# Query and key projections of the first block computed with dims on partitions, and their rotary turn made there

## The reference, cut to what matters

```python
proj = jnp.einsum('bsd,de->bse', xn, w_in)
q_a, k_a, v_a, q_r, k_r, v_r, g_r, gate_logits = jnp.split(proj, IN_SPLIT_POINTS, axis=-1)
def apply_rotary(t, cos, sin):
    t1, t2 = jnp.split(t.astype(jnp.float32), 2, axis=-1)
    c = cos[None, :, None, :]
    s = sin[None, :, None, :]
    return jnp.concatenate([t1 * c - t2 * s, t1 * s + t2 * c], axis=-1)
...
for g, (window, dilation) in enumerate(ATTN_PAIRS):
    o, l = dilated_window_attention(q_a[:, :, g], k_a[:, :, g], v_a[:, :, g], dilation, window // (2 * dilation))
...
mix_w = jax.nn.softmax(jnp.stack(lses, axis=0), axis=0)
y_att = jnp.einsum('gbsh,gbshd->bshd', mix_w, jnp.stack(outs, axis=0)).reshape(B, S, ATTN_OUT_W)
```

## Time and profile before

| | |
|---|---|
| median of 3 runs | 2767.23 us (2767.2 to 2769.93) |
| profiled execution | 2768.16 us, its span 2766.3 us |
| TensorE busy | 2609.0 us, 94% |
| VectorE, ScalarE, GpSimd busy | 1219.6, 880.6, 852.4 us |
| the four mixers end at | about 382 us of the span |

### The profile page before, as it was taken

The page is one execution under the profiler, slowest core; times in us unless marked ns, Lnnn a source line. Parts: engine busy times, 40 slices in busy tenths (PEclk is TensorE's granted clock), DMA queues, the critical chain, the costliest instruction groups (busy, mean ns, idle before and its releaser), DMA issues.

```text
span 2766.3 us, 36753 instructions
## 1 busy us (share of the span) xinstructions
PE 2609.0 (94%) x14332; PEld 1850.0 (67%) x14332; DVE 1219.6 (44%) x2420; ACT 880.6 (32%) x1671; POOL 852.4 (31%) x1166
## 2 busy tenths in 40 slices
PE   9999999999988888888888899999999999999999
PEld 7888777888533333334333367788888887888887
DVE  6433745225633333333333357553441565644422
ACT  4433335322211111111111144553332446433332
POOL 5343434552000000000000043345555435345554
PEclk9999999999999999999999999999999999999999
DMA  4223222336999999999999951122332221123322
GB/s 159 79 100 105 72 76 77 104 122 257 414 427 427 428 429 428 429 429 429 428 428 428 426 178 66 50 92 92 94 115 95 90 100 61 62 91 106 108 92 76
DMA packets 128151, 571.99 MB, mean 207 GB/s; under 512 B 11152, under 2 KB 58640, under 8 KB 102928
## 3 DMA queue, kind: packets, MB, share of 16 engines
q1 hardware_dynamic: 122768, 560.82, 51.0%
q10 hardware_dynamic: 5248, 9.32, 1.1%
HBM read 565.86 MB, written 4.26 MB: 206 GB/s over the span
## 4 chain that ended last, share of the span: by engine, by line
PE 68%; DMA 23%; DVE 5%; ACT 2%; issue 1%; POOL 0%; SPq 0%; ACTq 0%; DVEq 0%
PE ps L392 43%; DMA wide<-in_moe_w 16%; PE ps L1577 8%; DMA arena<-in_moe_w 7%; PE ps L2105 3%; PE ps L2084 2%; PE ps L2074 1%; PE ps L2125 1%; PE ps L673 1%; PE ps L708 1%; PE ps L689 1%; PE ps L2091 1%; PE ps L1353 1%; PE ps L937 0%; POOL ring_r L349 0%
## 5 line engine op out<-in xcount | busy, mean ns | idle before, releaser
L349 POOL TENSOR_TENSOR ring_r<-ring,ring_r 128x256 fp32r<-128x256 f32 (+2 forms) x1136 | 833.7, 773 | 1818.3 <-ACT ring_r L332 1818.3
L392 PE MATMUL ps<-xnT_r,ring_r 128*128 128x512 f32 (+1 forms) x1664 | 483.9, 374 | 0.0
L392 PE MATMUL ps<-ring_r,xnT_r 128*128 128x512 f32 (+1 forms) x1296 | 412.7, 389 | 3.0 <-DVE xn_r L3171 2.5
L392 PEld LDWEIGHTS ps<-xnT_r,ring_r 128*128 128x128 f32 x1664 | 304.4, 188 | 56.6 <-issue 1.3
L392 PE MATMUL ps<-ring_r,arena_r 128*128 128x512 f32 x1392 | 323.9, 391 | 0.0
L392 PE MATMUL ps<-xn_r,ring_r 128*128 128x512 f32 (+1 forms) x832 | 310.2, 373 | 0.0
L332 ACT ACTIVATE ring_r<-ring 128x1024 fp32r<-128x1024 f32 (+2 forms) x284 | 272.4, 1025 | 88.7 <-DMA ring<-in_w_down 67.4
L392 PEld LDWEIGHTS ps<-ring_r,arena_r 128*128 128x128 f32 x1392 | 259.9, 188 | 56.4 <-issue 2.2
L392 PEld LDWEIGHTS ps<-ring_r,xnT_r 128*128 128x128 f32 x1296 | 251.0, 200 | 49.9 <-issue 5.7
L2105 PE MATMUL ps<-wide,arena 128*32 128x512 f32 x752 | 192.0, 657 | 90.5 <-DMA wide<-in_moe_w 90.5
L2105 PEld LDWEIGHTS ps<-wide,arena 128*32 128x32 f32 x752 | 51.8, 118 | 229.5 <-issue 210.8
(11 more groups left out here) (407 smaller groups left out, 3491.2 us busy)
## 6 DMA issues: line engine op xcount, KB each, us to landing
wide<-in_moe_w SPq DMA_DIRECT2D x143, 2048.0 KB, 32.9
arena<-in_moe_w SPq DMA_DIRECT2D x46, 2048.0 KB, 32.9
ring<-in_w_in SPq DMA_DIRECT2D x22, 2048.0 KB, 8.3
ring<-in_w_up SPq DMA_DIRECT2D x20, 2048.0 KB, 8.6
ring<-in_w_down SPq DMA_DIRECT2D x10, 2048.0 KB, 7.8
ring<-in_w_in SPq DMA_DIRECT2D x16, 512.0 KB, 4.9
ring<-in_w_out SPq DMA_DIRECT2D x4, 2048.0 KB, 8.5
ring<-in_w_ret_branch SPq DMA_DIRECT2D x2, 2048.0 KB, 9.0
```

The source lines that it names most:

```text
L349: ins = nc.gpsimd.tensor_tensor(ring_r[:, q % 2, piece], ring[:, q % 2, piece], ring_r[:, 2 + q % 2, piece].bitcast(F32), ALU.subtract)
L392: ins = nc.tensor.matmul(bank, left, right, start=(start and k == 0), stop=(stop and k == 2))
```

## The change

Six projections, all query and key ones but the first mixer's query and the last mixer's key, become "crossed" jobs: the weights are the stationary operand and all 512 tokens the moving one, so that job b gives dims 128b to 128b+127 of all tokens, already turned. Their rots go. ScalarE first copies the four groups of 32 partitions, halves of a head swapped, into `X.swapped` (`swap_crossed_act`); then VectorE multiplies them by a sine table, multiplies the bank by the cosine table, and adds both into `qT` or `kT` (`rotate_crossed_dve`). The two tables of 512 columns, 512 KB together, are loaded into `rows[:, 3]` ahead of unit 1. The turn back of a tile stands six chunks after the values (before: directly behind them). From unit 1 on, high copies stand at chunk 5 of the second job and chunks 1, 3 and 5 of the third.

```diff
+        BACK = 6
...
-                            if 2 <= p <= pairs and tile_of_pair(self.attention, p - 2) is not None:
-                                yield "back", tile_of_pair(self.attention, p - 2)
...
-                        if pairs and off == 2 and p == pairs + 1:
-                            yield "back", NT - 1
+                        if pairs and off == BACK and 2 <= p <= pairs + 1 and tile_of_pair(self.attention, p - 2) is not None:
+                            yield "back", tile_of_pair(self.attention, p - 2)
...
+                    if toks == CROSSED:
+                        ins = products(ps[:, dense_bank(e), :], [xnT_high[:, c, :], h_low[:, c, :]], [w[:, c, i * P:(i + 1) * P] for w in chunks_of_unit(u)],
+                                       weights_left=True, **flags)
...
+        def rotate_crossed_dve(v, M, e, n):
...
+            v.wait_ge(Z.turned, M.rots0 + sum(r < n for r in M.roped) - (x == 0))
+            v.wait_ge(halves_swapped, y + 1)
+            nc.vector.tensor_tensor(swapped, swapped, X.sin_T, ALU.mult)
+            nc.vector.scalar_tensor_tensor(out=rot, in0=ps[:, dense_bank(e), :], scalar=M.scales[way], in1=X.cos_T, op0=ALU.mult,
+                                           op1=ALU.mult).then_inc(Z.taken_dve, 1)
...
+            nc.vector.tensor_tensor(dst, rot, swapped, ALU.add).then_inc(rotated, 1)
...
+        def swap_crossed_act(a, M, e, n):
...
+            a.wait_ge(Z.proj_ready, M.jobs0 + n + 1)
+            if y >= 2:
+                a.wait_ge(rotated, y - 1)
...
+            half = DH // 2
+            for at in range(0, P, half):
+                other = at ^ half
+                ins = nc.scalar.activation(X.swapped[y % 2][at:at + half], ps[other:other + half, dense_bank(e), :], ACT.Copy, scale=scale)
+            ins.then_inc(halves_swapped, 1)
+
+        HIGH_AT = ((1, 5), (2, 1), (2, 3), (2, 5))
...
-                    if i == 2 and c % 2:
+                    if u == 0 and i == 2 and c % 2:
                         high_act(a, u + 1, (c // 2,))
+                    elif u and (i, c) in HIGH_AT:
+                        high_act(a, u + 1, (HIGH_AT.index((i, c)),))
...
+            at, n = TABLES["rope_t"]
+            sp.dma_start(rows[:, 3], const[:, at:at + n]).then_inc(rope_loaded, 16)
```

More of the change, by code:

```diff
@@ L107, in tables @@
     parts["rel"] = np.concatenate([rel, from_middle * np.ones((P, 1))], 1)
+    turns = (np.arange(S, dtype=np.float32)[None] * np.tile(inv, P // inv.size)[:, None]).astype(np.float32)
+    signs = np.where(p % DH < DH // 2, -1.0, 1.0)
+    parts["rope_t"] = np.concatenate([np.cos(turns), signs * np.sin(turns)], 1)
     at = 0
@@ L592, in build @@
             assert lay.at == ARENA
+            cos_T, sin_T = rows[:, 3, 0:S], rows[:, 3, S:]
             merged_top = small[:, 32:64].rearrange("p (i h) -> p i h", i=NT)
@@ L612, in build @@
         FIRST_HALF, SECOND_HALF, WHOLE = slice(0, HALF), slice(HALF, P), slice(0, P)
-        ENDS = "ends"
+        ENDS, CROSSED = "ends", "crossed"
         end_tokens = extra_r[:, 0:2 * KC * P].rearrange("p (x c t) -> p x c t", x=2, c=KC)
@@ L818, in __init__ @@
                 self.attention, self.first, self.apart, self.leaves, self.merges = attention, first, apart, leaves, merges
-                self.roped = [n for n, (kind, _, _, _) in enumerate(jobs) if kind != "v"]
+                self.crossed = [n for n, job in enumerate(jobs) if job[3] == CROSSED]
+                self.roped = [n for n, job in enumerate(jobs) if job[0] != "v" and n not in self.crossed]
+                self.by_dve = sorted(self.roped + self.crossed)
                 self.entries = []
@@ L864, in steps @@
                         yield "merge", k - 3
-                assert not pairs or self.first + self.apart * (pairs + 1) + 2 < at
+                assert not pairs or self.first + self.apart * (pairs + 1) + BACK < at
             def job(self, e):
@@ L892, in mixer_of @@
             values = [ENDS] + [SHIFTED[i] for i in range(1, NT)] if g == 0 else [tokens(i, True) for i in range(NT)]
-            jobs = [(kind, base + j, i, tokens(i, False)) for j, kind in enumerate("qk") for i in range(NT)]
+            jobs = [(kind, base + j, i, tokens(i, False) if base + j == 0 else CROSSED) for j, kind in enumerate("qk") for i in range(NT)]
             jobs += [("v", base + 2, i, toks) for i, toks in enumerate(values)]
@@ L902, in mixer_ret @@
         def mixer_ret():
-            jobs = [(kind, U_REST + j, i, tokens(i, False)) for j, kind in enumerate("qvkv") for i in range(NT)]
+            jobs = [(kind, U_REST + j, i, CROSSED if kind == "q" else tokens(i, False)) for j, kind in enumerate("qvkv") for i in range(NT)]
             dsts = [X.vr_low[:, i, :] for i in range(NT)] + X.vr_high
@@ L948, in mixer_pe @@
                         pe.wait_ge(Z.turned_kept, M.rots0)
+                        pe.wait_ge(rotated, M.crossed0)
                         pe.wait_ge(Z.taken_act, M.acts0)
@@ L1008, in mixer_dve @@
                         last_merge_dve(v, link, k)
+        def rotate_crossed_dve(v, M, e, n):
+            x = M.crossed.index(n)
+            y = M.crossed0 + x
+            kind, _, b, _ = M.jobs[n]
+            way = "qk".index(kind)
+            rot, swapped = X.rot[:, x % 2, :], X.swapped[y % 2]
+            v.wait_ge(Z.proj_ready, M.jobs0 + n + 1)
+            if y == 0:
+                v.wait_ge(rope_loaded, 16)
+            v.wait_ge(Z.turned, M.rots0 + sum(r < n for r in M.roped) - (x == 0))
[3 more added lines that the diff above has]
+                                           op1=ALU.mult).then_inc(Z.taken_dve, 1)
+            v.wait_ge(Z.taken_dve, M.dves0 + M.by_dve.index(n) + 1)
+            dst = M.heads[way][:, b, :]
+            if M.permuted:
+                rot, swapped = (z.rearrange("p (k r) -> p r k", r=STRIDE) for z in (rot, swapped))
+                dst = dst.rearrange("p (r k) -> p r k", r=STRIDE)
+            nc.vector.tensor_tensor(dst, rot, swapped, ALU.add).then_inc(rotated, 1)
+            v.wait_ge(rotated, y + 1)
+        def swap_crossed_act(a, M, e, n):
+            y = M.crossed0 + M.crossed.index(n)
+            scale = M.scales["qk".index(M.jobs[n][0])]
+            a.wait_ge(Z.proj_ready, M.jobs0 + n + 1)
+            if y >= 2:
+                a.wait_ge(rotated, y - 1)
+            elif y == 0:
+                a.wait_ge(Z.roped, M.rots0 + len(M.roped))
+            half = DH // 2
[4 more added lines that the diff above has]
+        HIGH_AT = ((1, 5), (2, 1), (2, 3), (2, 5))
         def mixer_act(a, M):
@@ L1030, in mixer_act @@
                             a.wait_ge(Z.probs_turned, sum(len(chunks_of(g)) for g in ORDER))
+                            a.wait_ge(rotated, M.crossed0 + len(M.crossed))
                             at, n_rel = TABLES["rel"]
@@ L1035, in mixer_act @@
                         nc.scalar.activation(dst, ps[:, dense_bank(e), :], ACT.Copy).then_inc(Z.taken_act, 1)
+                    elif c == KC - 1 and M.entries[e][1] in M.crossed:
+                        swap_crossed_act(a, M, e, M.entries[e][1])
+                        if M.before is None and M.entries[e][1] == 2 * NT - 1:
+                            decays_act(a, 1)
                 elif what == "rot":
                     m = M.entries[k][1]
+                    way = "qk".index(M.jobs[M.roped[m]][0])
                     a.wait_ge(Z.turned, M.rots0 + m + 1)
-                    dst, src = M.heads[m // NT], ps[:, dense_bank(k), :]
+                    dst, src = M.heads[way], ps[:, dense_bank(k), :]
                     if M.permuted:
@@ L1318, in rest_pe @@
                         pe.wait_ge(Z.turned_kept, last.rots0 + len(last.roped))
-                        pe.wait_ge(Z.taken_act, last.acts0 + len(last.jobs) - len(last.roped))
+                        pe.wait_ge(rotated, last.crossed0 + len(last.crossed))
+                        pe.wait_ge(Z.taken_act, last.acts0 + len(last.jobs) - len(last.by_dve))
                     if s_ >= 2:
```

60 lines of the change are left out of this document (32 added, 28 removed).

## The result

The changed kernel takes 2784.81 us (median of 4 runs, 2784.12 to 2792.2), the kernel before 2767.22 beside it: the ratio is 1.0067, 95% interval 1.0055 to 1.008. It is 17.6 us slower; the forecast was 2770 in a range that ended at 2779.

A forecast was written before the change was run, and what follows sets the result against it. TensorE was taken as the only engine on the chain. Rots removed, waits in the second, third and last mixer: -10.6 + 1.9 + 1.9 + 9.6 = +2.8 us, arriving whole, so 2770 us, range 2762 to 2779.

The forecast's parts named there:

- What is removed: TensorE's chain in the mixers: 24 of 32 rots go at 0.44 us each, 10.6 us saved.
- 96 x 0.272: TensorE, the removed transposes: if each gave back its whole duration, 26.1 us would go and the sum end at 2754.
- The four copies: ScalarE, each crossed job: four copies of 32x512 take about 2.07 us, upper bound 2.34, lower 0.6.
- If the copies step by 0.6 or more: ScalarE's groups of 32x512: a sign that the forecast is wrong; it expected steps of 0.5 us.
- The rotation: VectorE, each crossed job: two multiplications and an addition take 2.2 us, bounded by 2.1 and 2.6.
- The waits of the middle mixers: Second and third mixer, values of pairs 1 and 2: TensorE waits 0.3 and 1.5 us, 1.9 us per mixer.
- The prediction's own walk: Queues walked through the second mixer: 1.9 us of waits; with copies of 2.34 and rotation of 2.6 it ends at +10.
- rival 2: Second and third mixer: ScalarE and VectorE in lockstep become the bound from copies of about 2.25 us, 2773 to 2781, chance 0.33.
- The last mixer: Values wait for the late merge: 3.7 us for tile 0, 3.1 tile 1, 2.7 tile 2, 0.1 last tile; sum 9.6.
- The clock is no part of the answer: TensorE in the stretches that the change touches: the granted clock is 1.00, so it gets no term.
- The banks, the table, the rest: Second mixer's start waits 0.7 us, the 0.61 behind the last goes, these cancel; 1.3 us of table load is hidden.
- The high copies: From unit 1 on: left in place they would cost some 2 us; the new, earlier place costs nothing.

The follow-up runs named there:

- e3: The changed kernel with one ScalarE copy of 128x512 for the four, halves not swapped (result not the reference's): 2769.53 us, 1.0003.
- e10: The changed kernel with the last mixer as before and the halves swapped on VectorE straight from the bank, without ScalarE: 2767.35 us, 0.9992.
- e12: The changed kernel with the last addition in natural token order, so tokens are wrongly ordered in the first two mixers: 2787.70 us, 1.0057.
- e4: The changed kernel with 20 short products that nothing reads ahead of each of the last mixer's three waits: 2785.00 us, 1.0056.
- e5: The changed kernel with 9 short products that nothing reads ahead of the waits at the values, middle mixers included: 2781.97 us, 1.0051.
- e13: e10 with the dense banks going on in turn from one mixer to the next: 2764.81 us, 0.9989.
- e11: The changed kernel with the high copies back in the third job's odd chunks: 2798.80 us, 1.0099.
- e1: The changed kernel with the turns of the last mixer alone back at their old chunks: 2775.89 us, 1.0026.
- e6: The changed kernel with the last mixer as before, its query uncrossed and its turns at the old place: 2778.05 us, 1.0038.
- e8: The changed kernel with a tile's merge issued at its turn back instead of at the end of the job: 2780.70 us, 1.0043.
- e2: The kernel before with only the turn back six chunks later in all mixers: 2777.60 us, 1.0030.
- e14: e13 with all turns at the old place, six chunks earlier: 2765.17 us, 0.9989.

## Why the prediction was wrong

**Where the 14.8 us are.** The forecast sum was +2.8, the measured difference 17.6. Without the rots the middle mixers lose 12.0 where 3.8 was forecast, 8.2 more, and the last 16.2 where 9.6 was, 6.6 more. Two steps of the prediction failed. The first took the four copies as overlapping (2.07 us for 2.39) and the rotation as 2.2 (2.8 on average in the second mixer), and so found ScalarE and VectorE just fast enough. The second put the clock at nothing.

**What is removed: right.** The rots gave about their 0.44 us on the chain. e3's middle mixers are 2.4 and 3.7 us shorter than before where 3.5 was forecast, e10's 3.2 and 3.7, and the start 2.0 where 1.8 was. That is far from 96 x 0.272.

**The four copies: mis-sized.** 2.07 us was taken; the runs show 2.39, above even the upper bound of 2.34. The step took the overlap of two 128-partition copies for copies of 32 partitions, and the nearer row, 0.585 for one of that shape, showed a whole duration. "If the copies step by 0.6 or more" stood in the prediction as a sign of being wrong, and it came true. The Trainium skill's 0.72 for a copy (ScalarE: Activation LUTs, Rules for kernel authors) is stated for an instruction whose bias is a pointer, which these copies don't have: the mean of 96 is 0.589.

**The rotation: mis-sized.** 2.2 was taken, 2.6 the bound; 2.8 is the mean of the second mixer, 2.3 that of the third. The multiplication L1035 takes 0.69 to 1.13 us, 0.80 on average; the strided addition takes 1.09 us, and 1.60 where GpSimd works. In e12, without the stride, the addition takes 0.69 beside an idle GpSimd and 1.21 beside a busy one. The Trainium skill (SBUF — State Buffer, SBUF: two separate sides) says that VectorE with two inputs in SBUF and GpSimd lock one shared port pair against each other, and the 0.69 and 1.21 agree. The stride's 0.4 is a second cost beside it, shown by 1.09 against 0.69.

**The waits of the middle mixers: right in place, wrong in size.** 1.9 and 1.9 were forecast, with the first pair's wait 0.3 and the second's 1.5. Measured are 2.18 and 1.06 in the second mixer, 2.15 and 0.72 in the third, and another 1.9 for low parts of weights; 6.8 and 5.2 are lost in all. The prediction's own walk ended at +10 with 2.34 and 2.6, and it gave 3.6 us for each 0.3 on the copies; with 2.39 that is about +10.6 instead of +2.8, an estimate. The mechanism is that of rival 2: its condition, four copies at 2.25 us or more, came true, though 2785 lies above its range too. e3 and e10 show it: one copy for four, or no ScalarE in the chain, and these waits go.

**The last mixer: place right, sum short.** Tile 1's wait was forecast at 3.1 and is 3.08. Tile 2's is 2.59 against 2.7. Tile 0's was 3.7, "between 0 and 5", and is 5.27, by the copies once more (0.92 in e3); the last tile's 0.1 is 0.8. So 11.7 against 9.6. The chain of work in the changed kernel shows tile 1's as worked out, from the key's rotation through the merge to the values:

```profile
336.50 0.61 DVE rows L570
...
337.13 0.70 DVE rows L991
...
339.39 0.69 DVE arena L1188
340.08 0.61 DVE rows L1189
...
340.83 1.09 PE ps L715 x16
```

**"The clock is no part of the answer": this step failed too.** It was read from stretches in which TensorE never stood, and the change makes it stand. Of the last mixer's 16.2 us about 4.9 are clock by the windows, and 11.7 are waits. In e4 and e5 the last mixer is 1.7 and 2.4 us shorter, with products that themselves cost something. The account can be closed from the profile alone. Waits of 4.6, 3.4 and 11.7 us and a clock worth 1.6, 1.6 and 4.9 (0.97 over 55 us in each middle mixer) make 27.8; less the rots of these three mixers, 8.8, and the bank's 0.7, that is 18.3 of the 19.4 us that they lose. The remaining 1.1 us I can't place.

**The banks, the table, the rest.** The 0.7 stands at the head of the second mixer as forecast and the one behind the last mixer is gone. The table is hidden, as far as the start shows: the first scores come 2.0 us earlier, and the rots removed there give 1.8. The 32 transposes forecast are left (L951). A crossed product costs what a plain one does: e10 and e13 have 80.8 us in the third mixer, 84.5 less the eight rots. The difference arrives whole behind the mixers in the changed kernel, 17.4 of 17.6. That it must always arrive whole is not so: e13 hands on 4 of 10 us.

**The high copies: result right, reason too small.** "Left where they were they would cost some 2 us": e11 shows 14.0. The new place was costed at nothing and costs 1.9 us of waits for L353, and three of its copies, 2.84 us, stand in the chain between exponentials and halves. The walk that gave the 2 was the walk that found ScalarE too free.

**What stays open.** The middle mixers of the same code come in two lengths, 88.9 and 86.2 (after, e1, e5 nearly) or 89.9 and 87.8 (e4, e6, e8 nearly); which one goes with where the clock falls. In the shorter it is 0.97 from 85 to 140 (1.00 in e5), in the longer 0.95 from 140 to 176. This is e6, a window and two lines of TensorE's timeline:

```profile
140.00:176.00 36.00, 33.38 (x166) 31.21 (x165) 9.35 (x11) 18.91 (x28) 24.57 (x32) 0.95 0.16 59
...
128.51 1.09 PE L715 MATMUL ps<-rows,arena 128*64 128x128 f32 x16 [2.18 <-ACT arena L782]
...
144.60 1.47 PE L715 MATMUL ps<-rows,arena 128*64 128x128 f32 x16 [2.62 <-ACT arena L782]
```

In the changed kernel the clock is low behind the first wait, and the second wait is then 1.06 us instead of e6's 2.62. In e6 it is low behind the second, and no further wait takes up the loss. e5, with the clock at 1.00 behind both, has the shorter lengths, as this reading wants. What decides behind which wait the clock falls, these traces don't show.

The turn back six chunks later also takes 4.1 us from the release of the bank in the middle mixers. e2 and e14 show that this place makes no difference there without ScalarE's copies; with them the old place was not tried in the middle mixers. The share of the 0.4 us of stride in the whole is open too.

## What to carry to other kernels

When a change moves work off the engine that bounds the kernel, follow the loop between the engines that take it, and add up its length: four copies on ScalarE in that loop cost 10.7 us that VectorE alone, with more work per job, did not, and one copy in their place did no harm in the middle mixers. A walk through the queues whose result hangs on a duration needs the nearest row's duration, not the best one, and where it ends in a wait of some us on the bounding engine, the clock behind the wait is a term of the sum. When an edit early in the program gives less at the end than at its own stage, look for one stall without a releaser before explaining it with the edit.

## What was not expected of the hardware

- ScalarE copies of 32 partitions of 512, PSUM to SBUF: 0.589 us each, 2.39 for four in a row, each as long as a copy of 128 partitions (0.598, L782); no overlap between them. On VectorE four multiplications of that shape took 2.84.
- A two-input VectorE addition with a stride of 16 bytes between elements: 1.09 us instead of 0.69, and 1.60 instead of 1.21 beside a busy GpSimd.
- Behind some waits of 2.2 to 5.3 us TensorE's granted clock falls from 1.00 to 0.50, and 16 products take 1.5 to 2.1 us instead of 1.09. Behind others of the same length it does not: 1.09 behind 3.08 us at 340.83, and 1.09 behind e6's 2.18. Where the next wait ends by another engine's work, the low clock costs next to nothing (e5).
- TensorE can stand for 5 us in a later stage because of an edit far ahead: with none of the work there changed, 16 short products made the stall appear in one kernel (+10.0 us with their own time) and go in another (-5.2), and 32 made it go too. The Trainium skill (Runtime: NRT & Kernel Launch, Instruction fetch mechanics) says that instructions are fetched in blocks and in sequence, and that a taken branch to a block that isn't there stalls until it is. That would fit; that this is the cause is not shown here, though the place of the instructions is what fits all the kernels.
